# Every natural main product of a two-block transformer kernel made as two products of 256 weight columns

## The reference, cut to what matters

```python
# first block (depth 1)
z = rms_norm(x) @ w_in                       # 2048 -> 11264 columns
#   HGRN2 scan (8 heads of 128) on hq, hf, hi, hg; banded attention (16 heads of 64) on aq, ak, av
merged = sigmoid(gate_a) * (y_a @ w_branch_a) + sigmoid(gate_b) * (y_b @ w_branch_b)
h = x + merged @ w_out                       # 2048 -> 2048
u = rms_norm(h)
h = h + square(relu(u @ w_up)) @ w_down      # 2048 -> 8192 -> 2048
x = rms_norm(h)
# second block: 16 meta tokens ahead, 272 tokens
proj = rmsnorm(concat(meta, x)) @ w_in_2     # 2048 -> 6656 columns
#   grouped-query attention with axial rope (8 heads), differential attention with a distance bias (8 heads)
out = h + rmsnorm(concat(ya, yb) @ w_out_2)  # 2048 -> 2048
```

## Time and profile before

| | |
|---|---|
| Runs (three) | 1893.53, 1893.94, 1894.71 us |
| Span of the profiled execution, first to last instruction | 1893.3 us |
| Mean granted TensorE clock | 0.999 of full |
| TensorE products (MATMUL) / loads (LDWEIGHTS) | 13432 / 13432 |
| TensorE busy, products / loads | 99% / 92% |
| VectorE / ScalarE / GpSimd busy | 58% / 47% / 8% |
| Chain that ended last | TensorE 97% of the span; L446 58%, L458 33% |

### The profile page before, as it was taken

One profiled execution on the slowest core, in us unless ns is written; L12 is line 12 of the kernel. 1 busy time (PEld: TensorE's weight loads), 2 busy tenths in 40 slices (PEclk: granted clock), 3 DMA queues, 4 the chain that ended last, 5 costly groups with the idle time before them and its releaser, 6 DMA issues.

```text
span 1893.3 us, 33876 instructions
## 1 busy us (share of the span) xinstructions
PE 1879.6 (99%) x13432; PEld 1743.7 (92%) x13432; DVE 1101.4 (58%) x1270; ACT 889.3 (47%) x1171; POOL 143.6 (8%) x122
## 2 busy tenths in 40 slices
PE   9999999999999999999999999999999999999998
PEld 9989998999999889988998899899889999899986
DVE  6556766667655555545445445445565556767664
ACT  6544444455544445443444344334454355664543
POOL 2001322411001100000010000000010000000000
PEclk9999999999999999999999999999999999999999
DMA  8566565566565656656665665566556655354454
GB/s 270 184 181 177 181 179 178 165 200 180 168 231 191 214 186 179 194 198 192 196 192 193 194 191 194 194 190 190 189 185 181 179 170 150 105 147 144 156 190 143
DMA packets 176434, 346.47 MB, mean 183 GB/s; under 512 B 10976, under 2 KB 11184, under 8 KB 175776
## 3 DMA queue, kind: packets, MB, share of 16 engines
q1 hardware_dynamic: 174176, 337.76, 57.2%
q0 software_dynamic: 2128, 6.82, 1.4%
HBM read 342.44 MB, written 2.10 MB: 182 GB/s over the span
## 4 chain that ended last, share of the span: by engine, by line
PE 97%; DVE 1%; ACT 0%; DMA 0%; issue 0%; SPq 0%; DVEq 0%; ACTq 0%
PE ps L446 58%; PE ps L458 33%; PE ps L548 1%; PE ps L781 1%; DVE wlo L1301 1%; PE ps L771 1%; PE ps L748 1%; PE ps L791 0%; DMA raw<-in_w_in_dram 0%; ACT whi L899 0%; PE ps L476 0%; PE ps L759 0%; PE ps L599 0%; PE ps L591 0%; DVE xlo L1323 0%; PE ps L610 0%
## 5 line engine op out<-in xcount | busy, mean ns | idle before, releaser
L1301 DVE TENSOR_TENSOR wlo<-raw,whi 128x1024 fp32r<-128x1024 f32 x631 | 796.5, 1268 | 698.1 <-ACT whi L899 697.1
L899 ACT ACTIVATE whi<-raw 128x1024 fp32r<-128x1024 f32 x631 | 664.5, 1058 | 886.3 <-PE ps L446 551.5
L446 PE MATMUL ps<-xhi,whi 128*128 128x256 f32 (+1 forms) x1904 | 542.2, 285 | 0.4 <-DVE wlo L1301 0.3
L446 PE MATMUL ps<-xhi,wlo 128*128 128x256 f32 (+1 forms) x1904 | 531.3, 279 | 0.0
L446 PE MATMUL ps<-xlo,whi 128*128 128x256 f32 x1664 | 462.5, 278 | 0.0
L446 PEld LDWEIGHTS ps<-xhi,whi 128*128 128x128 f32 x1904 | 359.1, 189 | 9.3 <-issue 6.7
L446 PEld LDWEIGHTS ps<-xhi,wlo 128*128 128x128 f32 x1904 | 357.8, 188 | 0.0
L446 PEld LDWEIGHTS ps<-xlo,whi 128*128 128x128 f32 x1664 | 313.4, 188 | 1.5 <-issue 0.7
L446 PE MATMUL ps<-x2hi,whi 128*128 128x256 f32 x1024 | 282.8, 276 | 0.0
L446 PE MATMUL ps<-x2hi,wlo 128*128 128x256 f32 x1024 | 282.7, 276 | 0.0
L446 PE MATMUL ps<-x2lo,whi 128*128 128x256 f32 x1024 | 282.7, 276 | 0.0
(11 more groups left out here) (373 smaller groups left out, 2370.6 us busy)
## 6 DMA issues: line engine op xcount, KB each, us to landing
raw<-in_w_in_dram SPq DMA_DIRECT2D x279, 512.0 KB, 3.8
raw<-in_w_up_dram SPq DMA_DIRECT2D x128, 512.0 KB, 3.7
raw<-in_w_down_dram SPq DMA_DIRECT2D x128, 512.0 KB, 3.7
raw<-in_w_out_dram SPq DMA_DIRECT2D x64, 512.0 KB, 3.8
raw<-in_w_branch_a_dram SPq DMA_DIRECT2D x16, 512.0 KB, 4.9
raw<-in_w_branch_b_dram SPq DMA_DIRECT2D x16, 512.0 KB, 3.8
x_nat<-in_x_dram SPq DMA_DIRECT2D x4, 512.0 KB, 7.4
rel<-in_rel_turned_dram POOLq DMA_DIRECT2D x8, 256.0 KB, 4.3
```

Source lines behind the costliest of these rows:

```text
L446: ins = mm(outs[b], w[:, k % SLOTS, j, cols], v, start=start, stop=last and j == CK - 1 and i == 2, skip_group_check=True)
L899: f(whi[:, k % SLOTS], raw[:, k % SLOTS], ACT.Copy).then_inc(whi_ready, 1)
L1301: tt(wlo[:, k % SLOTS], raw[:, k % SLOTS], whi[:, k % SLOTS], ALU.subtract).then_inc(wlo_ready, 1)
```

## The change

In `chunk_n` each product of 512 weight columns becomes two of 256, made one after the other with the same stationary block, into the two halves of the same PSUM bank. Only the first half of the first product of a bank carries `start`. Nothing else is changed; lines behind L458 lie two lines later.

```diff
@@ -455,9 +455,11 @@
                     for t in halves:
                         toks = slice(t * P, (t + 1) * P)
                         for i, (v, w) in enumerate(((xh, whi), (xh, wlo), (xl, whi))):
-                            ins = mm(ps[:, 2 * s + t, :], v[:, kt, toks], w[:, k % SLOTS, j, :],
-                                     start=first and j == 0 and i == 0,
-                                     stop=last and j == CK - 1 and i == 2, skip_group_check=True)
+                            for c in range(2):
+                                cols = slice(c * CW // 2, (c + 1) * CW // 2)
+                                ins = mm(ps[:, 2 * s + t, cols], v[:, kt, toks], w[:, k % SLOTS, j, cols],
+                                         start=first and j == 0 and i == 0 and c == 0,
+                                         stop=last and j == CK - 1 and i == 2, skip_group_check=True)
                 if NT - 1 in halves:
                     ins.then_inc(pe_done, 1)
                 return ins
```

## The result

The changed kernel takes 1909.5 us (median of five runs, 1908.94 to 1911.3); the kernel before, on the same chip, 1893.53 us (1892.09 to 1894.71). The ratio is 1.0084, with a 95% interval of 1.0072 to 1.0096: slower by 0.84%, where 0.3% faster was forecast and 1903 us was the upper end of the range.

The account below looks back on a forecast made before the run. TensorE, hardly ever waiting, was taken to bound the kernel by products times pace. Faster products (-5.7 us) and handovers (-0.2) took the span from 1893.3 to 1887.4 us; the median 0.6 above gave 1888.0 us, range 1886.5 to 1903.

Parts of the forecast that it names:

- The bound: Whole kernel: TensorE, busy 99% of the span and hardly waiting, sets the time as number of products times pace.
- The count: Natural chunks: 2688 products of 512 columns become 5376 of 256, giving 16120 products on the page.
- the loads: Natural chunks: each half brings its own load, 2688 more, hidden within the 113.4 ns per product.
- the chunk pipeline: Chunk release to ScalarE and VectorE: every 2.72 instead of 2.75 us, already met in turned stretches, so no wait.
- instructions: TensorE: 5376 more instructions; fetches take 0.4% of the DMA engines, so no cost.
- PSUM: Natural chunks: successive products alternate between the halves of a bank; no cost expected.
- The price of the added products: 5376 split products at the faster 113.4 ns rather than 117.8: 2.1 ns won per old product, 5.7 us in all.
- The turned products: Unedited 256-column pieces with roles exchanged: expected unchanged, to within 0.03 us at handovers.
- The handovers: Seven places where a natural piece runs into a turned one: about 0.03 us each should vanish, 0.2 us.
- Rival 2: Split natural products lock at the slower pace, 6.7 ns each: +18.0 us, 1911.9 us if all; chance 0.20.
- The kindred case of rival 1: Only the six natural pieces behind L476 transposes lock slow: 4.6 us, 1892.6 us; chance 0.20 together with nothing won.
- The rule of the Trainium skill: Every product costs a fixed 2.5 ns besides its columns: splitting adds 6.7 us, about 1900.6 us.

Follow-up runs that it names:

- half by half: The changed kernel with all three parts of one half made before the three of the other; 1912.27 us beside 1894.22 for the kernel before.

## Why the prediction was wrong

**The bound** (TensorE alone, no waits, a matter of pace): right, and it stayed so.

**The count, the loads, the chunk pipeline, instructions, PSUM**: right. 16120 products and loads; no wait grew by more than 0.2 us; the order of the halves doesn't matter (half by half).

**The price of the added products.** This is the step that failed: "I take the faster, because it is the pace of the long pieces that run into the natural ones and out of them". Both paces were known from the earlier trace rows, and the faster gave -5.7 us. What the rows could not show is why the long turned pieces were fast: the three of 768 all follow wide natural products, and in the four kernels in which at least a chunk of wide products stood ahead of them all twelve were fast. At these handovers the change took away the very products that had left the stream fast. The other reason in the same sentence, that 1920 of the products follow a turned piece directly, named a link that held (the pace was kept there every time), but what is kept can be the slow one. For the pieces behind small products, half of all split products at 117.8 ns (1056 behind transposes, 480 behind the scan), the step had no row at all, and why they come out slow stays open. In place of the faster pace: 3072 of 5376 split products at 117.8 ns. Against half a wide product, 114.45 ns, these cost 3072 x 3.35 = 10.3 us, and the 2304 at 113.4 ns bring 2304 x 1.05 = 2.4 us; the net of 7.9 is near the 7.6 us of the sum over the pieces.

**The turned products**: "the pieces of turned products are unchanged" failed with it, 7.0 us on pieces of which no line was edited. For the 3.4 us of the 768 at 1084.53 us the reason is the same and shown. For the 3.2 us of the 720, and with it the slow start of the first w_down piece, it is open: in the run with some chunks left wide the 720 stayed slow with a wide chunk not far ahead of it; with w_out wide but for its first group it was fast, and also with three more transposes at each block.

**The handovers**: forecast to save 0.2 us. They are where the pace is passed on or lost. From turned to split natural it was kept every time. From split natural in w_down to the long turned pieces it was exchanged, fast for slow and slow for fast, in 23 of the 24 cases in the changed kernel and the seven runs with narrow products on both sides (three cases each; the exception is 1086.65 us in the run with one wide product midway, where slow stayed slow). By this rule the feed-forward part, which has three such handovers, can't be fast throughout in the changed form. The short turned pieces of 48 products don't follow it: all 21 of them (three in each of the seven kernels with narrow products on both sides there) stand behind a slow natural piece, the one at 150.52 us stayed slow every time, the one at 341.69 us turned fast every time, the one at 728.64 us stayed slow in six of seven. That a wide chunk at the long handovers undoes the flip is shown by the pair of versions that differ in nothing else: 3.3 us under and 8.3 us over the kernel before on the same chip, with the pieces as shown.

**Rival 2** named what came true, a new stream at the slower pace, though not why, with 1911.9 us for all products slow and 1899.9 for half. It was given too little, 0.20, and it priced the natural products alone: with 57% of them slow its own figures give 1888.0 + 3072 / 2 x 8.8 ns = 1901.5 us, the slow turned pieces add 7.0, and 1908.5 us is within a microsecond of the measured time. As the share and the 7.0 are measured ones, this checks the account and not the rival. The reason it was held against it, that the stream leaves the slow pace within some six products behind natural ones, was true of the long handovers from wide products only. Its reading of the two rows as a cost per product is wrong: split products run at 113.4 ns too.

**The kindred case of rival 1**, the six pieces behind transposes slow, came true in itself, and was not the whole.

The rule of the Trainium skill that stood beside rival 2 (TensorE: Matmul & The Clock Gate, section Back-to-back issue gap), a fixed part of 2.5 ns per product, gave 1900.6 us. That section gives the formula for the gap of an isolated product and says that it is off for a stream of loads and products, which this is; the prediction left that out. The sign was right and the reason isn't what the runs show: by that rule the version with 1788 products split would lose 4.5 us, an estimate from its figure, and it wins 3.3.

## What to carry to other kernels

Where a stream of short products bounds a kernel, its pace may have more than one stable value, and an edit can change it in stages that it doesn't touch: divide length by count for every piece of the chain before and after, the unchanged ones first. A pace read from rows is evidence for an edit only with what stands ahead of those rows. A gain of 2 ns per product was real here, and was to be had by making it only where the stream is entered fast and leaving one chunk in the wide form at each of the three long handovers.

## What the runs showed of the hardware that was not expected

- Products of 256 columns in fp32r, each with its load, at the 2.4 GHz clock (granted 1.00 in both kinds of stretch): 113.4 or 117.8 ns in the long pieces, nothing between but in the first products of a piece. Products of 512 columns: 228.9 ns, in every run. The state is kept over 768 products and from turned to natural products; from the natural pieces of w_down to turned ones it flips, 23 of 24 times, and at the short handovers it flipped in 8 of 21. A single step can't tell the two paces apart in these views, which round to 0.01 us; length divided by count can.

- Pieces ahead of 131 us differ between executions of kernels with the same code there: the turned one at 30 us takes 29.94 or 31.09 us, the one at 62 us 41.02 or 42.60 us, and the piece behind the one at 62 us inherits its pace. That is 1.2 to 3.8 us, the size of the scatter between the runs of one kernel (1908.94 to 1911.3 us). The 144 turned products at 381 us, which follow three transposes of the kernel's own `shift_phase`, took 16.96 us in seven of the thirteen profiled executions and 16.34 us in six; the kernel before is thus not free of this either. From 530 us on the main pieces of the changed kernel and of the run with another part order agree to a hundredth of a microsecond.
- What physically distinguishes the two states, why the exchange from natural to turned flips them in the feed-forward part and the other doesn't, and why split products behind transposes nearly always lock slow, stays open. How many neighbouring products share a stationary block, how often the half of the PSUM bank changes, and the tile at the handover are excluded by the runs above; a shared block as such is not, since every narrow stream here has it. Edits also shift the instructions behind them; their number alone doesn't set the pace, for with 25 more transposes the feed-forward pieces came out as in the changed kernel.
